# Stores of one head pair's output before or behind the next head pair's loads in SyncE's program

## The reference, cut to what matters

```
h   = modulate(rmsnorm(x), ...)
z   = h @ w_in                       # 2304 columns: heads of kinds A, B, D and a Fourier group
o_a = neighbourhood attention        # A: 4 heads, 2-D window with bias, plus 512 cached keys
o_b = differential attention         # B: 4 heads, two softmaxes each
o_c = Fourier mixing
o_d = windowed attention with sink   # D: 4 query heads, 2 key heads
x   = x + gate * (concat(o_a, o_b, o_c, o_d) @ w_out)
x   = x + gate * (relu(rms(x) @ w1)**2 @ w2)
```

## Time and profile before

| | |
|---|---|
| median of 3 runs | 3759.15 us (3758.63 to 3759.62) |
| profiled execution, its time | 3757.04 us |
| its span, first to last instruction | 3755.7 us |
| busy share: PE, DVE, ACT, POOL | 95%, 55%, 21%, 29% |
| mean granted PE clock | 0.978 |

### The profile page before, as it was taken

How to read it: one execution, slowest core, us unless ns; L and a number is a source line. 1 busy time by engine, 2 the same in 40 slices (tenths; PEclk the granted TensorE clock), 3 DMA queues, 4 the chain that set the end, 5 groups by cost and what they waited for, 6 DMA issues and landing times. The chain is left out here.

```text
span 3755.7 us, 48530 instructions
## 1 busy us (share of the span) xinstructions
PE 3574.8 (95%) x19394; PEld 2725.4 (73%) x19394; DVE 2082.9 (55%) x3234; ACT 797.7 (21%) x1284; POOL 1073.6 (29%) x718
## 2 busy tenths in 40 slices
PE   6999999889999999999989999988899999999998
PEld 4688444447888888888868864444488888888886
DVE  5232676653656666666573247765446555455455
ACT  3111454441200000000031125544321000000003
POOL 0010487752211111111131127777231111111113
PEclk8999999999999999999999999999999999999999
DMA  6754354434112212212215454343511011111111
GB/s 219 257 181 134 81 130 109 131 106 167 51 60 60 79 49 69 79 41 77 69 56 161 149 155 108 84 128 107 193 33 57 23 45 45 34 34 45 34 34 57
DMA packets 267721, 350.48 MB, mean 93 GB/s; under 512 B 66879, under 2 KB 194065, under 8 KB 267369
## 3 DMA queue, kind: packets, MB, share of 16 engines
q1 hardware_dynamic: 236560, 332.75, 28.5%
q10 hardware_dynamic: 30936, 14.64, 1.8%
HBM read 279.99 MB, written 72.16 MB: 94 GB/s over the span
## 5 line engine op out<-in xcount | busy, mean ns | idle before, releaser
L2426 PE MATMUL bank<-h_hi,w_hi 128*128 128x512 f32 (+1 forms) x2496 | 904.7, 362 | 30.6 <-issue 23.5
L2427 PE MATMUL bank<-h_lo,w_hi 128*128 128x512 f32 (+1 forms) x2496 | 888.9, 356 | 0.0
L2428 PE MATMUL bank<-h_hi,w_lo 128*128 128x512 f32 (+1 forms) x2496 | 888.7, 356 | 0.0
L2244 DVE SCALAR_TENSOR_TENSOR xT<-bank,mods,xT 128x512 f32<-128x512 f32 (+1 forms) x816 | 533.9, 660 | 267.9 <-PE bank L2428 255.8
L2426 PE MATMUL bank<-m_hi,w_hi 128*128 128x512 f32 (+1 forms) x1536 | 555.1, 361 | 16.3 <-DVE xT L2244 16.1
L2426 PEld LDWEIGHTS bank<-h_hi,w_hi 128*128 128x128 f32 x2496 | 475.0, 190 | 113.0 <-issue 41.7
L2428 PE MATMUL bank<-m_hi,w_lo 128*128 128x512 f32 (+1 forms) x1536 | 549.9, 358 | 0.0
L2427 PE MATMUL bank<-m_lo,w_hi 128*128 128x512 f32 (+1 forms) x1536 | 549.2, 358 | 0.0
L2427 PEld LDWEIGHTS bank<-h_lo,w_hi 128*128 128x128 f32 x2496 | 475.4, 190 | 72.5 <-issue 5.3
L2428 PEld LDWEIGHTS bank<-h_hi,w_lo 128*128 128x128 f32 x2496 | 474.8, 190 | 67.8
L940 POOL TENSOR_SCALAR w_hi<-stage 128x2048 fp32r<-128x2048 f32 x90 | 173.3, 1926 | 1054.6 <-issue 528.2
(11 more groups left out here) (216 smaller groups left out, 4115.8 us busy)
## 6 DMA issues: line engine op xcount, KB each, us to landing
stage<-in_w_mlp SPq DMA_DIRECT2D x64, 1024.0 KB, 5.2
nx_w<-in_w_ada SPq DMA_DIRECT2D x16, 1536.0 KB, 9.4
stage<-in_w_in SPq DMA_DIRECT2D x18, 1024.0 KB, 6.3
ada_h<-in_w_ada SPq DMA_DIRECT2D x16, 1024.0 KB, 8.4
rope_t<-in_k_rope SPq DMA_DIRECT2D x28, 512.0 KB, 4.9
rden<-s_rden ACTq DMA_DIRECT2D x28, 320.0 KB, 4.6
ada_w<-in_w_ada SPq DMA_DIRECT2D x4, 2048.0 KB
stage<-in_w_out SPq DMA_DIRECT2D x8, 1024.0 KB, 6.1
```

The lines of the kernel that those rows point to most:

```text
L2244: dve.scalar_tensor_tensor(out=x, in0=bank[:, bk, :n], scalar=mods[l][:, gate + k, cd:cd + 1], in1=x, op0=ALU.mult, op1=ALU.add).then_inc( ...
L2426: x = pe.matmul(out, a_hi, b_hi, start=first, stop=False)
L2427: pe.matmul(out, a_hi, b_lo, start=False, stop=False)
L2428: return x, pe.matmul(out, a_lo, b_hi, start=False, stop=last)
```

## The change

The three `store_out` of pair 4 no longer stand between the row sums of jobs 15 and 16. They stand behind `load_head` and `load_values` of pair 7, ahead of the row sums of job 18. The stores of pairs 5, 6 and 7 stay where they were.

```diff
@@ -1301,6 +1301,9 @@
                     load_head(sp, l, v + 1)
                     if VALUES_FIRST[v + 1]:
                         load_values(sp, l, v + 1)
+                    if v + 2 == NV:
+                        for cc in range(NCH):
+                            store_out(JOBS[(v - 2) * NCH][0], JOBS[(v - 2) * NCH][1], cc)
                 if v == 1:
                     for tab in (na_q, na_k):
                         flat = tab.rearrange("p x n -> p (x n)")
@@ -1329,7 +1332,7 @@
                 if kind == "A" and h2 == 0:
                     load_fourier_early()
                 denominators_out(v * NCH)
-                if v - 1 in PAIRS:
+                if v - 1 in PAIRS and v + 3 != NV:
                     for cc in range(NCH):
                         store_out(JOBS[(v - 1) * NCH][0], JOBS[(v - 1) * NCH][1], cc)
                 if kind == "A" and h2 == 0:
```

## The result

The changed kernel is slower.

| | median | before beside it | ratio (95% interval) |
|---|---|---|---|
| changed kernel | 3780.73 us (3774.1 to 3781.93, 4 runs) | 3759.39 us | 1.0053 (1.0041 to 1.0065) |
| the same, run again | 3771.39 us (3771.26 to 3779.82, 5 runs) | 3757.67 us | 1.0038 (1.0025 to 1.0050) |
| kernel before, run again as if changed | 3761.02 us | 3757.67 us | 1.0003 (0.9992 to 1.0014) |

A forecast was written before the change was run, and what follows sets the result against it. PE, busy 95% of the span, was taken as the bound. Later start +8.7 and +8.35, old holes -5.15 and -4.8, clock -0.5 each gave +3.05 us a layer, +6.1 in all: 3765 us, range 3754 to 3774.

The forecast's parts named there:

- The loads start 9.5 us earlier and k no longer holds PE: SyncE's queue, pair 7's loads: issued from about 718.85, k there at 727.5; PE's old hole goes, -5.15 and -4.8 us.
- A new wait of ACT takes its place, since chunk 0 can't be stored before the loads are through: ACT at chunk 2, slot 75: stops from about 720.8 to 736.4; chance 0.56 that this replaces PE's wait for loads.
- The landing of chunk 0: Store behind pair 7's loads: landed at 736.4 in the first layer, 2569.5 in the second; the early end was 730.9.
- so PE can start the values of slot 76 ... It started them at 729.46: +8.7 us: PE, values of slot 76: start at about 738.15, +8.7 us in the first layer and +8.35 in the second.
- DVE works ahead through the hole: DVE, slots 76 and 77: does not stop, bias additions ready, so ACT has slot 77 done by about 741.4.
- The maxima row costs nothing once the loads are early: ACT's row, sent at about 741.5, has over 4 us to land: costed at nothing, up to 1 us a layer if late.
- The clock: PE's half clock behind the hole: 2.4 us lost as now, taken as 0.5 us a layer less; ends none and 3.4.
- POOL's backlog: POOL's additions for slots 76 to 78: done at 749.6, 4.35 us later than now, covered; otherwise 1.3 us a layer.

The follow-up runs named there:

- after_own_buffer: The changed kernel, order untouched, with buffers of its own for chunk 2 of pair 4: 0.9969 of the kernel before, 3749.39 us.
- row_sums_first: The changed kernel, with ACT copying the row sums of job 17 before rounding chunk 2 of pair 4: 1.0016 of the kernel before, 3767.68 us.
- chunk0_early: The changed kernel, with chunk 0 of pair 4 stored in its old place, chunks 1 and 2 behind the loads: 0.9974 of the kernel before, 3750.63 us.
- chunk2_later3: The changed kernel, with ACT's rounding of chunk 2 of pair 4 three slots later: 0.9972 of the kernel before, 3747.70 us.
- loads_before_sums: Against the kernel before: pair 7's loads right behind chunk 0's old-place store, then job 16's row sums, chunks 1 and 2: 0.9966, 3747.03 us; again 0.9973.
- stores_behind_sums: Against the kernel before: pair 4's three stores behind the row sums of job 16 but ahead of pair 7's loads: 1.0011, 3763.32 us.

## Why the prediction was wrong, point by point

- **The loads start 9.5 us earlier and k no longer holds PE.** Right: k is not waited for in any kernel that moves the loads forward.
- **A new wait of ACT takes its place, since chunk 0 can't be stored before the loads are through.** Right. after_own_buffer took that wait away and nothing else, and the kernel was 0.31% faster instead of 0.38 to 0.53% slower.
- **The landing of chunk 0.** Forecast 17.6 us behind the first load's issue. In the repeated run ACT went on at 736.80, 17.25 us behind that issue at 719.55, having waited 15.11 us; in the first run at 746.04, 21.35 us behind it. In the second layers, where 17.2 was forecast, it was 19.3 us in the first run and 18.8 in the repeated one. So the term was right once and short by 1.6 to 3.8 us three times, and each microsecond of it is one of hole. The spread is mostly in the loads, not in the store. In the first layer SyncE reached the store 12.1 us behind the first load's issue in the first run (736.81 less 724.69) and 8.7 us in the repeated one (728.22 less 719.55), with 9.25 forecast; from there to ACT's restart it took 9.2 and 8.6 us, with 8.3 forecast. Why the loads take longer stays open.

```profile
736.80 0.42 ACT L1739 ACTIVATE ao_hi<-o_ad 128x256 fp32r<-128x256 f32 x1 [15.11 <-DMA s_o<-ao_lo]
```

```profile
719.55 0.35 SPq L887 DMA_DIRECT2D q<-s_qD  x1
...
728.22 3.29 SPq L1288 DMA_DIRECT2D s_o<-ao_hi  x1
```

- **The step that failed: "so PE can start the values of slot 76 ... It started them at 729.46: +8.7 us".** The prediction listed the row sums of job 17 among what ACT does late, but asked only who waits for the exponentials. PE never got to those values. Behind the rounding in ACT's program stands the copy of the row sums of job 17, and the PSUM bank (a piece of the memory that PE writes its results to) that it empties is the next one that PE wants, for the second piece of slot 76, which it had started at about 724.7. PE thus stops 4.8 us sooner than at 729.46. It restarts 0.9 us sooner too, since no exponential need be done. From the rows on which the prediction stood the sum would have been: PE restarts at 736.4 + 0.1 + 0.41 + 0.4 = 737.3, +12.6 us, less 5.15, or +7.5 us a layer and +15 us in all, 3774. The late landing, 5.9 us over both layers of the first run, makes up the rest to 20 us. row_sums_first shows the step by itself: with the copy ahead of the wait PE stops where the prediction had it, and the loss is 0.16% instead of 0.38 to 0.53.
- **DVE works ahead through the hole.** Also wrong for slot 77, by the same step: with PE stopped ahead of slot 77's scores there was nothing to add biases to, and ACT waited 5.21 us more for DVE behind the hole. In row_sums_first it holds.
- **The maxima row costs nothing once the loads are early.** Right in the changed kernel: PE does not wait for the row at 758.94, 2.9 us after it was sent (756.07). Wrong in the faster kernels: 0.7 to 2.1 us a layer of waiting for it are left in chunk0_early, after_own_buffer, chunk2_later3 and loads_before_sums.
- **The clock.** Forecast as 0.5 us less lost per layer. In the first layer of the repeated run the clock is at half when PE restarts, at 737.54, and back at full at about 742.2, by the windows below; 4.7 us at half are 2.3 us lost, the same as before and not less. In the second layer it is at half from 2575.89 to about 2582, which is 3.1 us lost, 0.7 more than before.

```profile
736.00:738.00 2.00, 0.46 (x2) 0.29 (x2) 0.00 (x0) 1.20 (x3) 0.71 (x1) 0.50 0.71 271
...
740.00:742.00 2.00, 2.00 (x8) 0.36 (x4) 0.00 (x0) 0.00 (x0) 1.86 (x2) 0.50 0.00 0
742.00:744.00 2.00, 2.00 (x16) 1.44 (x16) 0.74 (x2) 0.00 (x0) 0.59 (x1) 0.94 0.00 0
...
2580.00:2582.00 2.00, 2.00 (x10) 1.48 (x10) 0.00 (x0) 0.00 (x0) 0.94 (x1) 0.50 0.00 0
2582.00:2584.00 2.00, 2.00 (x17) 1.04 (x16) 1.72 (x3) 0.40 (x1) 0.00 (x0) 1.00 0.00 0
```

- **POOL's backlog.** POOL's additions were never named as the releaser of a hole of PE in this place; the term was not needed.

## What to carry to other kernels

When an engine that works in order gets a new wait, list everything behind it, also what only empties a bank or a buffer, and price the stall at the earliest of their users; here the one that carries the data was not the first. A store that frees a ring buffer needed soon should not go behind a large load in the same queue: here one chunk of three stayed ahead, and then the same move was worth 0.3%. A buffer of its own for that chunk, or its rounding three slots later in the waiting engine, did the same.

## What the runs showed of the hardware that was not expected

The time that the same nine loads take varies from run to run and from layer to layer. In stores_behind_sums PE used k 12.7 us after the first issue (740.84 less 728.11) and in the second layer 12.2 us after it; in the kernel before it was 8.7 us. There the first load is issued 0.05 us behind the end of a store's issue, but that is not enough to make the loads slow. In loads_before_sums it is issued just as close behind one, and the view of single lines, whose landing times are compared only with each other here, has q's loads landed 9.1 us after issue in the first layer and 12.6 in the second. It has 14.0 and 13.1 us in stores_behind_sums, 9.1 and 8.6 in the kernel before, 12.6 and 10.0 in the first profile of the changed kernel and 8.6 and 10.0 in its repeated run:

```profile
720.62 0.43 SPq L1288 DMA_DIRECT2D s_o<-ao_lo  x1
721.10 1.22 SPq L887 DMA_DIRECT2D q<-s_qD  x1
...
DMA to landing us min/median/max: 9.1/9.1/9.1
```

What makes the loads slower was not tried and stays open.

A row of 2 KB on ACT's queue, sent while SyncE's loads fill the DMA engines, released PE 8.3 us later in the kernel before, 10.8 us later in stores_behind_sums, where the loads were slower (743.23 less 732.42), and 4.2 us later in chunk0_early, where the loads were further on. That fits a row whose landing waits for another queue's transfers; no run tests it by itself.
